# Two-block transformer on one core: mixer preparation reordered, last expert gate turned earlier, sums of squares by column groups

## Chip, cores and metric

The kernel runs on one core of a Trainium2 chip, as one program that computes the whole forward pass. The metric is the device time of one execution in microseconds; the figure of a kernel is the median of its runs. Lower is better.

## What is computed

The input is 512 tokens of width 1024, all in fp32. A first block has two layers (block-sparse attention, then an HGRN2 recurrence), each followed by a mixture of 16 experts with two chosen per token. A second block has, for l = 0 and 1: a gated feed-forward, a mixer of three parts (RWKV-7, sparse latent attention, retention) on one common projection, a second feed-forward. The functions that the change reaches, cut:

```python
# mixture of experts: 512 tokens x 2 experts, sorted by expert, padded to blocks of 128 rows
yb = (silu(xblk @ w1[e]) * (xblk @ w3[e])) @ w2[e]          # gate and up, then down
out = zeros((n + 1, d)).at[buf_t].add(yb * buf_w[:, None])  # back to the tokens
# rms norm ahead of the HGRN2 layer and the others: needs sum(x*x) of every token
y = x * rsqrt(mean(x * x, -1) + eps)
# RWKV-7 (6 heads of 64): low-rank products give decay, a, gate; then a recurrence over tokens
# retention (4 heads of 64), by chunks of 128 tokens
z1, z2 = z[..., :half], z[..., half:]                        # q and k are rotated
rot = concatenate([z1 * cos - z2 * sin, z1 * sin + z2 * cos])
scores = einsum('bnhd,bmhd->bhnm', qc, kc) * intra[None]
inner = einsum('bhnm,bmhe->bhne', scores, vc)
y = y * rsqrt(mean(y * y, -1) + eps); y = silu(g) * y        # per head, then gated
# sparse attention: for every token the 128 best keys by an index score, softmax over them
score = einsum('bqh,bqhs->bqs', iw_b, relu(einsum('bqhd,bsd->bqhs', iq_b, ik)))
_, idx = lax.top_k(where(visible, score, -inf), topk)
```

## The kernel before

**One in-order queue per engine.** The program is written out by hand: each engine (pe = TensorE, act = ScalarE, dve = VectorE, pool = GpSimd, and the DMA queue of SyncE) has one function per stage, which issues its instructions in order, waits for marks that other engines set (`pe.wait_ge(*dve.at(...))`) and sets its own (`.then_inc(*pe.mark(...))`). There is no scheduler: an instruction that waits holds up all behind it on its engine. `edge(eng, name)` (L230) sets a mark of the engine and waits until all the other engines have passed theirs of that name. PSUM banks go round in rings: `take` hands out a bank, and `before` lists what has to have emptied it.

**Weaving.** Where two parts of the work are independent, each is a generator, and `weave` (L2662) calls them in turn, one step each, in the order in which they are given; a generator given as `beside` is advanced once every `every` turns, and what is left of it is taken up later. The same weave stands in the functions of all three engines, so that their queues have the same order.

**Precision.** Matrices are multiplied as sums of three fast products: each operand is split into a rounded part (hi, by ScalarE: `cut_hi` L328, `moe_hi` L1310) and a remainder (lo, by VectorE: `cut_lo` L338, `moe_lo` L1317), and TensorE adds hi*hi, lo*hi and hi*lo (L357 to L359, L1423 to L1425, L1441 to L1443). Weights stream from HBM, three pieces ahead.

**The expert stages** (`moe_pe` L1346, `moe_act` L1498, `moe_dve` L1577). The chosen rows lie in NB = 23 blocks. In step t of the loop TensorE turns the rows of block t, turns the gated product of block t-2 (`turn_a`: four transposes into a bank), runs gate and up of block t-1, and then the down product of block t-2 (`down`, 24 products of 512 columns in four quarters k). In the last step, t = NB + 1, only `turn_a(NB - 1)` and `down(NB - 1)` are left. ScalarE and VectorE walk through the pieces of weights (i counts them in a step) and insert their other work at given i: x_hi, a_hi (L1521), y (L1534, empties the down product), silu; and x_lo, a_lo (L1711), gated (L1717). After the last block y is stored, GpSimd gathers the rows of every token (L1774), VectorE mixes them into four groups of 128 tokens (L1747), TensorE turns each group with eight transposes (L1465), and VectorE adds them to x (L1753, eight instructions of 128x512, from the last group on).

**Sums of squares ahead of the HGRN2 layer** (`hg_sums_pe` L1833, `hg_sums_act` L1846, `hg_proj_act` L1906). ScalarE squares each of the eight 128x512 parts of x (L1855). TensorE multiplies each in four 128x128 blocks with a single column of ones, 32 pairs of weight load and product in all, each shown as two records (L1842 x64), and gets the sum of a token in one of 128 rows; ScalarE takes the root (L1909).

**The mixer** (`mix_pe`, `mix_act`, `mix_dve` L3778 to L3808). It has six parts in order:

- Projections (`mix_proj_*` from L2712): 26 products with streamed weights in `m.order` (27 in mixer 1), one per step s. The index scores and the choice of the keys (`index_*` L2986 to L3059) are woven in, `m.pace[s]` steps of their generator after each projection. VectorE shifts RWKV's projections by one token (`shifted`), two steps after each; at the end it passes the edge "shift", and only then takes what is left of the choice (L3054 to L3059 are its last instructions).
- Preparation: `rwkv_in_*` (L3200) and `ret_*` (L2869) woven together, RWKV first. For RWKV: tanh and sigmoid of the low-rank inputs (L3268, L3269), the nine low-rank products (L3227, outer loop over the three kinds j on their 32 or 64 rows, inner loop over three parts i), the sums of kk squared, cumulative decays, four exponentials of them on ScalarE, among them E3 of the decay less its last step (L3326 on VectorE makes that difference), turned copies and a bonus (L3248). For retention: four rotation products into the ring ps6 (L2876), VectorE's rotation (L2952), scores (L2890) and their decay (L2970), values (L2903), the squares' sums and root, a factor that ScalarE copies wide (L2939) and TensorE spreads (L2686 x16), and two closing products on VectorE (L2983).
- Heads (`head_*` from L3397, first product L3416): three pairs of heads woven together in 16 turns, with one step of the attention (`dsa_*` L3061) every two turns.
- Chunks (`chunks_*` L3543): 27 turns of the RWKV recurrence, woven with the rest of the attention while it lasts.
- Output (`mix_out_*` L3680).

The lines of the steps on the shift edge and the weave:

```python
            edge(dve, n + " shift")                  # in mix_proj_dve, at its end
            for _ in side:                           # side: what is left of the choice
                pass
...
            weave(rwkv_in_dve(v, m), ret_dve(v, m))  # in mix_dve
            edge(dve, m.name + " heads")
```

## Time and profile before

| | |
|---|---|
| median of 3 runs | 4387.55 us (4386.54 to 4388.22) |
| the profiled execution's own time | 4376.6 us |
| its span | 4374.8 us |
| mean granted TensorE clock | 0.966 |
| TensorE busy | 4126.4 us, 94% |
| VectorE busy | 2631.0 us, 60% |
| ScalarE busy | 1965.7 us, 45% |
| GpSimd busy | 167.7 us, 4% |
| DMA | 635.88 MB, 145 GB/s in the mean |

The span runs from the first to the last instruction of the profiled execution; its own time is 1.8 us longer, and the median of the unprofiled runs 10.95 us above that. The granted clock is TensorE's, as a share of full speed: 1.0 is 2.4 GHz, 0.5 is 1.2 GHz. In the rows PE is TensorE's matmul, PEld its weight load, DVE is VectorE, ACT ScalarE, POOL GpSimd; L3219 is line 3219 of the kernel. "x <- y" after a wait names who released it. Times of rows are microseconds from the start of the span unless marked ns.

### The profile page before, as it was taken

The numbers are of one execution on the slowest core, as the hardware profiler recorded it, in microseconds if no ns is written. First come the engines' busy times: TensorE is split into PE (matmuls) and PEld (weight loads), VectorE is DVE, ScalarE is ACT, GpSimd is POOL, SyncE is SP. The second block draws the span as 40 slices with busy tenths as digits, with TensorE's granted clock in tenths as the row PEclk, the third lists the DMA queues.
The fourth block names the chain that finished last, engine by engine and source line by source line (L and its number), as shares of the span: only waits on it lengthen the run. The fifth ranks groups of instructions, "written<-read, shape, count | busy, mean of one in ns | idle before, by whom it ended". The sixth has DMA issues, their size and how long they took to land.

```text
span 4374.8 us, 61152 instructions
## 1 busy us (share of the span) xinstructions
PE 4126.4 (94%) x25548; PEld 3197.4 (73%) x25548; DVE 2631.0 (60%) x4330; ACT 1965.7 (45%) x3254; POOL 167.7 (4%) x151
## 2 busy tenths in 40 slices
PE   7889999998998999989999978999999999889998
PEld 4656778886777788867777656777777776567776
DVE  4467669995346599964445865544544457655444
ACT  3345448884345488852223343322322233443222
POOL 0000000000011000010000000000000000000000
PEclk9999999998999999989999989999999999899999
DMA  5155269994210599942222101222222221012221
GB/s 206 63 193 188 78 256 426 414 403 159 87 59 2 232 426 410 407 170 97 94 87 101 45 3 40 96 95 83 94 98 86 85 107 44 2 40 78 96 96 68
DMA packets 61853, 635.88 MB, mean 145 GB/s; under 512 B 6743, under 2 KB 7127, under 8 KB 27016
## 3 DMA queue, kind: packets, MB, share of 16 engines
q1 hardware_dynamic: 46024, 575.34, 33.4%
q0 software_dynamic: 8928, 32.51, 2.0%
q10 hardware_dynamic: 6624, 24.12, 1.4%
q8 instruction: 201, 3.29, 0.3%
q14 instruction: 76, 0.62, 0.0%
HBM read 601.49 MB, written 30.45 MB: 144 GB/s over the span
## 4 chain that ended last, share of the span: by engine, by line
PE 83%; DVE 9%; ACT 5%; issue 1%; DMA 1%; POOL 0%; POOLq 0%; SPq 0%; DVEq 0%; ACTq 0%
PE ps L357 14%; PE ps L358 14%; PE ps L359 14%; PE ps L1425 4%; PE ps L1424 4%; PE ps L1423 4%; PE ps L1441 2%; PE ps L1443 2%; PE ps L1442 2%; PE ps L1013 2%; DVE wbuf_r L338 1%; PE ps L573 1%; PE ps L378 1%; PE ps L379 1%; PE ps L380 1%
## 5 line engine op out<-in xcount | busy, mean ns | idle before, releaser
L358 PE MATMUL ps<-arena_r,wbuf_r 128*128 128x512 f32 x2848 | 1139.4, 400 | 0.0
L338 DVE TENSOR_TENSOR wbuf_r<-slot,wbuf_r 128x512 fp32r<-128x512 f32 (+1 forms) x832 | 594.6, 722 | 675.6 <-ACT wbuf_r L328 666.7
L357 PE MATMUL ps<-hT_r,wbuf_r 128*128 128x512 f32 x2144 | 868.7, 405 | 17.9 <-DVE arena_r L475 12.2
L359 PE MATMUL ps<-hT_r,wbuf_r 128*128 128x512 f32 x2144 | 853.3, 398 | 0.0
L328 ACT ACTIVATE wbuf_r<-slot 128x512 fp32r<-128x512 f32 (+1 forms) x832 | 506.4, 614 | 714.0 <-PE ps L359 605.0
L358 PEld LDWEIGHTS ps<-arena_r,wbuf_r 128*128 128x128 f32 x2848 | 537.2, 189 | 134.7 <-issue 4.6
L357 PEld LDWEIGHTS ps<-hT_r,wbuf_r 128*128 128x128 f32 x2144 | 405.6, 189 | 143.1 <-DVE arena_r L475 20.7
L359 PEld LDWEIGHTS ps<-hT_r,wbuf_r 128*128 128x128 f32 x2144 | 406.1, 189 | 101.5
L357 PE MATMUL ps<-arena_r,wbuf_r 128*128 128x512 f32 x704 | 279.1, 396 | 0.0
L359 PE MATMUL ps<-arena_r,wbuf_r 128*128 128x512 f32 x704 | 279.1, 396 | 0.0
L1317 DVE TENSOR_TENSOR wbuf_r<-arena,wbuf_r 128x1024 fp32r<-128x1024 f32 x164 | 195.7, 1221 | 44.3 <-ACT wbuf_r L1310 43.8
L1317 DVE TENSOR_TENSOR arena_r<-arena,arena_r 128x1024 fp32r<-128x1024 f32 x164 | 196.8, 1226 | 5.9 <-ACT arena_r L1310 5.2
L2497 ACT ACTIVATE arena_r<-arena 128x512 fp32r<-128x512 f32 x88 | 55.6, 632 | 309.6 <-DVE arena L2533 309.6
L1310 ACT ACTIVATE wbuf_r<-arena 128x1024 fp32r<-128x1024 f32 x164 | 174.1, 1063 | 44.2 <-PE ps L1425 25.2
L1310 ACT ACTIVATE arena_r<-arena 128x1024 fp32r<-128x1024 f32 x164 | 171.3, 1064 | 36.1 <-PE ps L1425 19.2
L2492 ACT ACTIVATE arena<-arena 128x512 f32<-128x512 f32 x88 | 55.6, 632 | 237.8 <-DVE arena L2527 237.8
L1317 DVE TENSOR_TENSOR wbuf_r<-slot,wbuf_r 128x1024 fp32r<-128x1024 f32 x112 | 133.7, 1221 | 38.4 <-ACT wbuf_r L1310 38.2
L359 PEld LDWEIGHTS ps<-arena_r,wbuf_r 128*128 128x128 f32 x704 | 132.6, 188 | 32.4
L357 PEld LDWEIGHTS ps<-arena_r,wbuf_r 128*128 128x128 f32 x704 | 132.6, 188 | 32.4
L1423 PE MATMUL ps<-wbuf_r,hT_r 128*128 128x512 f32 x368 | 148.4, 403 | 3.1 <-DVE hT_r L1706 3.1
L1310 ACT ACTIVATE wbuf_r<-slot 128x1024 fp32r<-128x1024 f32 x112 | 118.8, 1063 | 70.5 <-DMA slot<-in_moe 45.4
L1425 PE MATMUL ps<-arena_r,hT_r 128*128 128x512 f32 x368 | 146.1, 397 | 0.0
(541 smaller groups left out, 7072.7 us busy)
## 6 DMA issues: line engine op xcount, KB each, us to landing
arena<-in_moe SPq DMA_DIRECT2D x82, 2048.0 KB, 11.3
slot<-in_moe SPq DMA_DIRECT2D x54, 2048.0 KB, 11.7
slot<-in_gu SPq DMA_DIRECT2D x44, 2048.0 KB, 7.5
slot<-in_ada SPq DMA_DIRECT2D x20, 2048.0 KB, 7.6
slot<-in_down SPq DMA_DIRECT2D x16, 2048.0 KB, 7.5
slot<-in_win SPq DMA_DIRECT2D x12, 2048.0 KB, 7.6
yrow<-arena ACTq DMA_DIRECT2D x46, 512.0 KB, 10.5
slot<-in_hgrn SPq DMA_DIRECT2D x8, 2048.0 KB, 7.9
```

The source lines that it names most:

```text
L328: a.activation(hi[:, 0:w], src[:, off:off + w], ACT.Copy).then_inc(*act.mark(c.name, "hi", i))
L338: v.tensor_tensor(lo[:, 0:w], src[:, off:off + w], hi[:, 0:w].bitcast(F32), ALU.subtract) \
L357: p.matmul(bank, hi[:, cs], rh[:, k, :], start=k == 0, stop=False, skip_group_check=True)
L358: p.matmul(bank, hi[:, cs], rl[:, k, :], start=False, stop=False, skip_group_check=True)
L359: t = p.matmul(bank, lo[:, cs], rh[:, k, :], start=False, stop=k == kt - 1, skip_group_check=True)
L1013: t = p.matmul(o, pb[:, half, k * 128:k * 128 + 128], att.diag[u % 2][:, half, :], start=True, stop=True, skip_group_check=True)
L1310: a.activation(hi, src[:, j * 1024:j * 1024 + 1024], ACT.Copy).then_inc(*act.mark(n, "hi", *piece))
L1317: v.tensor_tensor(lo, src[:, j * 1024:j * 1024 + 1024], hi.bitcast(F32), ALU.subtract) \
L1423: p.matmul(bank, xh[:, ks], hi[:, cs], start=k == 0, stop=False, skip_group_check=True)
L1424: p.matmul(bank, xl[:, ks], hi[:, cs], start=False, stop=False, skip_group_check=True)
L1425: t = p.matmul(bank, xh[:, ks], lo[:, cs], start=False, stop=k == 7, skip_group_check=True)
L1441: p.matmul(bank[hf], ah[:, ks], hi[:, cs], start=k == 0, stop=False, skip_group_check=True)
```

## The change

1. `edge` is split: `others_at` only waits. In a mixer VectorE sets its own "shift" mark ahead of its work for the last projection, at s = len(m.order) - 1, and waits for the others' where it did before. What is left of the choice of keys is handed on and woven beside the preparation on VectorE.
2. In the preparation retention comes first and RWKV second, on all engines. The rotation products go to the two banks of the ring `hold`, two and two, a step apart. The low-rank products have the parts i outside and the kinds j inside; tanh and sigmoid of their inputs move to step 20 of the projections. The sums of kk squared come one step earlier. The exponential E3 and VectorE's difference for it are gone: `ah` is computed from E1, shifted by one token inside each chunk of 64, by two instructions. Buffers move (`m.vmix` in three parts, `m.rR`), and with `m.vmix` one product of VectorE becomes three in mixer 1.
3. The end of retention (ScalarE's wide copy, the spread on TensorE, VectorE's closing products) becomes a generator of its own, `ret_end_*`, two steps chained ahead of the attention, beside the heads.
4. In the expert stages the gate of the last block is turned at k == 2 of the down product of the block before; its a_hi and a_lo follow at i == 9 of step t = NB.
5. After each of the first three token groups TensorE runs four products of 128 columns whose result is not used.
6. The sums of squares ahead of HGRN2 become eight products with a 32-column matrix of ones, each into the 32-row group k % 4 of one bank, the first four starting and the last four adding; ScalarE copies the bank, and four products with one column each (`corners`) add the four groups for every token.

```diff
 def edge(eng, name):
     eng.also("edge", name)
+    others_at(eng, name)
+
+def others_at(eng, name):
     for other in (pe, act, dve, pool):
...
 # moe_pe: down(b), and the loop over t
     for k in range(4):
+        if b == NB - 2 and k == 2:
+            turn_a(b + 1)
...
-    if 0 <= t - 2:
+    if 0 <= t - 2 < NB - 1:
         turn_a(t - 2)
...
     for dt in range(8):
         p.transpose(out[dt][:, t4 * 128:t4 * 128 + 128], ...)
+    if t4 < 3:
+        busy_pe(p, out[7][:, 384:512], 4)
 # moe_act (moe_dve the same with a_lo)
-    if i == 2 and t > 1:
+    if i == 2 and 1 < t <= NB:
         a_hi(t - 2)
+    if i == 9 and t == NB:
+        a_hi(t - 1)
 # hg_sums_pe
+    bank = hg.ps.take("rows", (act, "hgrn", "x rows"))
...
+    for k in range(8):
+        c = k % 4 * 32
+        pe.wait_ge(*act.at("hgrn", "x sq", k))
+        p.matmul(bank[c:c + 32, :], ones[:, 0:32], m.xg[k // 2 % 2][:, k % 2 * 512:k % 2 * 512 + 512], start=k < 4,
+                 stop=k > 3, ...).then_inc(*pe.mark("hgrn", "x sums", k))
...
-    for k in range(8):
-        pe.wait_ge(*act.at("hgrn", "x sq", k))
-        for t4 in range(4):
-            at = k % 2 * 512 + t4 * 128
-            t = p.matmul(bank[:, t4:t4 + 1], m.xg[k // 2 % 2][:, at:at + 128], ones[:, 0:1], ...)
+    pe.wait_ge(*act.at("hgrn", "x rows"))
+    for t4 in range(4):
+        t = p.matmul(bank[:, t4:t4 + 1], m.gsb[1][:, t4 * 128:t4 * 128 + 128], corners, start=True, stop=True, ...)
+    t.then_inc(*pe.mark("hgrn", "x col"))
 # hg_proj_act
     act.wait_ge(*pe.at("hgrn", "x sums", 7))
+    a.activation(m.gsb[1], hg.ps.buf("rows"), ACT.Copy).then_inc(*act.mark("hgrn", "x rows"))
+    act.wait_ge(*pe.at("hgrn", "x col"))
 # mix_plan
-    m.rR = m.rot.rearrange("p a b -> p (a b)")
+    m.rR = hflat[:, 1536:2560]
...
-    m.vmix, m.vdiff = m.bon, vfirst
+    m.vmix, m.vdiff = [hT[:, 6, :], hT[:, 7, :], late[:, 3584:4096]], vfirst
 # mix_proj_act
+    if s == 20:
+        act.wait_ge(*dve.at(n, "shifted", 9))
+        a.activation(m.lo[0:32, :], m.lo[0:32, :], ACT.Tanh).then_inc(*act.mark(n, "lo", 0))
+        a.activation(m.lo[64:128, :], m.lo[64:128, :], ACT.Sigmoid).then_inc(*act.mark(n, "lo", 2))
 # mix_proj_dve
+    if s == len(m.order) - 1:
+        dve.also("edge", n + " shift")
...
-    edge(dve, n + " shift")
-    for _ in side:
-        pass
+    others_at(dve, n + " shift")
+    return side
 # ret_pe (ret_dve yields at the same places)
     for z in range(4):
-        bank = m.ps6.take(("rot", z), (dve, n, "rot", z))
+        bank = m.hold.take(("rot", z), (dve, n, "rot", z))
...
-    yield
+        if z % 2:
+            yield
...
+def ret_end_pe(p, m):
     for i in range(2):
-        bank = m.ps6.take(("ret spread", i), (dve, n, "ret done", i))
+        bank = m.dps.take(("ret spread", i), (dve, n, "ret done", i))
...
         pe.wait_ge(*act.at(n, "ret R"))
         spread_pe(p, bank, m.rR, 2, i).then_inc(*pe.mark(n, "ret spread", i))
     yield
+    yield
 # rwkv_in_pe (rwkv_in_act the same)
-    for j, rows in ((1, slice(32, 64)), (0, slice(0, 32)), (2, slice(64, 128))):
-        for i in range(3):
+    for i in range(3):
+        for j, rows in ((1, slice(32, 64)), (0, slice(0, 32)), (2, slice(64, 128))):
...
-    yield
     bank = take("kk sums", (act, "kk root"))
...
+    yield
 # rwkv_in_act: Tanh, Sigmoid and this go
-    act.wait_ge(*dve.at(n, "less"))
-    a.activation(m.ah, m.ah, ACT.Exp, scale=-rate).then_inc(*act.mark(n, "E3"))
 # rwkv_in_dve
-    tt(m.ah, m.cum, m.lw, ALU.subtract, n, "less")
...
-    dve.wait_ge(*act.at(n, "E3"))
-    v.scalar_tensor_tensor(out=m.ah, in0=m.kkn, scalar=-1.0, in1=m.ah, op0=ALU.mult, op1=ALU.mult)
+    v.scalar_tensor_tensor(out=by_chunk(m.ah)[:, :, 1:64], in0=by_chunk(m.kkn)[:, :, 1:64], scalar=-1.0,
+                           in1=by_chunk(m.E1)[:, :, 0:63], op0=ALU.mult, op1=ALU.mult)
+    v.tensor_scalar(by_chunk(m.ah)[:, :, 0], by_chunk(m.kkn)[:, :, 0], -1.0, None, ALU.mult)
 # mix_pe (mix_act and mix_dve alike)
-    weave(rwkv_in_pe(p, m), ret_pe(p, m))
+    weave(ret_pe(p, m), rwkv_in_pe(p, m))
     edge(pe, m.name + " heads")
-    dsa = dsa_pe(p, m)
+    dsa = chain(ret_end_pe(p, m), dsa_pe(p, m))
     weave(*[head_pe(p, m, i) for i in range(3)], beside=dsa, every=2)
 # mix_dve
-    weave(rwkv_in_dve(v, m), ret_dve(v, m))
+    weave(ret_dve(v, m), rwkv_in_dve(v, m), beside=choice)
```

## Rows read from the trace of the kernel before

**Rows 1.** The page, part 1: busy us, share of the span, instructions

```profile
PE 4126.4 (94%) x25548; PEld 3197.4 (73%) x25548; DVE 2631.0 (60%) x4330; ACT 1965.7 (45%) x3254; POOL 167.7 (4%) x151
```

**Rows 2.** Preparations: us, then busy PE, PEld, DVE, ACT, POOL; PEclk, DMA share, GB/s

```profile
2499.00:2569.70 70.70, 58.29 (x216) 31.64 (x217) 41.68 (x66) 33.02 (x46) 0.00 (x0) 0.70 0.04 16
...
3703.80:3780.50 76.70, 63.72 (x222) 33.16 (x222) 45.81 (x64) 33.70 (x48) 0.00 (x0) 0.68 0.04 14
```

**Rows 3.** Waits (total us, times, longest): TensorE, whole run; VectorE, preparation 0; 1

```profile
PE ps L3219 <- DVE arena L3056: 10.8, 2, 6.6
...
DVE arena L2952 <- PE ps L2876: 13.7, 1, 13.7
DVE wbuf L2970 <- PE ps L2890: 6.6, 5, 2.6
...
DVE arena L2979 <- ACT arena L2936: 2.0, 1, 2.0
...
DVE wbuf L2970 <- PE ps L2890: 8.0, 4, 4.5
```

**Rows 4.** Order of time on TensorE, mixer 0: start us, us, line, xcount

```profile
2500.02 12.77 PE L3227 MATMUL ps<-arena,small 32*128 32x512 f32 x18
2512.72 6.39 PE L2876 MATMUL ps<-arena,const 128*128 128x512 f32 x8
...
2532.21 1.97 PE L2903 MATMUL ps<-wbuf,arena 128*64 128x512 f32 x4
```

**Rows 5.** Order of time, mixer 0: what the change takes out or moves

```profile
2527.98 1.76 DVE L3326 TENSOR_TENSOR slot<-slot,arena 128x1536 f32<-128x1536 f32 x1
...
2568.87 0.69 DVE L2983 TENSOR_TENSOR hT<-hT,ps 128x512 f32<-128x512 f32 x1 [1.02 <-PE ps L2686]
...
2565.05 3.78 PE L2686 MATMUL ps<-const,arena 128*128 128x128 f32 x16 [1.74 <-ACT arena L2939]
```

**Rows 6.** Order of time: bonus products of both mixers; ScalarE pieces, table load

```profile
2539.95 2.84 PE L3248 MATMUL ps<-arena,const 128*128 128x512 f32 x6
...
3748.54 5.43 PE L3248 MATMUL ps<-arena,const 128*128 128x512 f32 x6 [3.71 <-DVE arena L3364]
...
2475.49 0.63 ACT L328 ACTIVATE wbuf_r<-slot 128x512 fp32r<-128x512 f32 x1 [2.19 <-PE ps L359]
...
2499.60 1.28 ACT L3269 ACT_TABLE_LOAD   x1
```

**Rows 7.** Busy time by stretch: mixer 0, heads, chunks with attention, chunks after it

```profile
2569.70:2637.40 67.70, 54.38 (x2192) 45.45 (x2192) 42.28 (x104) 26.36 (x61) 0.00 (x0) 1.00 0.04 8
2637.40:2690.50 53.10, 50.67 (x504) 37.36 (x504) 29.70 (x83) 24.56 (x67) 0.00 (x0) 1.00 0.09 36
2690.50:2702.10 11.60, 6.57 (x216) 5.70 (x212) 6.99 (x15) 1.00 (x2) 0.00 (x0) 1.00 0.01 1
```

**Rows 8.** Last expert of stage 0 in order of time; page row L1317

```profile
1013.10 0.68 DVE L1717 TENSOR_TENSOR arena<-arena,ps 128x512 f32<-128x512 f32 x1
...
1020.33 0.77 PE L1441 MATMUL ps<-wbuf_r,arena_r 128*128 128x512 f32 x1 [3.50 <-DVE arena_r L1711]
...
1027.45 1.08 ACT L1534 ACTIVATE arena<-ps 128x512 f32<-128x512 f32 x2 [7.99 <-PE ps L1443]
...
1032.61 0.94 POOL L1774 DMA_INDIRECT arena<-yrow,arena  x1 [85.20 <-DMA yrow<-arena]
...
L1317 DVE TENSOR_TENSOR wbuf_r<-arena,wbuf_r 128x1024 fp32r<-128x1024 f32 x164 | 195.7, 1221 | 44.3 <-ACT wbuf_r L1310 43.8
```

**Rows 9.** End of stage 0 in order of time: token groups, squares, spread

```profile
1049.70 5.36 DVE L1753 SCALAR_TENSOR_TENSOR xT<-ps,modv,xT 128x512 f32<-128x512 f32 x8 [0.57 <-PE ps L1465]
...
1049.18 1.97 PE L1465 MATMUL ps<-const,arena 128*128 128x128 f32 x8 [0.72 <-DVE arena L1747]
1051.26 13.79 PE L1842 MATMUL ps<-const,arena 128*128 128x1 f32 x64
1066.43 2.04 PE L1882 MATMUL ps<-arena,const 128*128 128x512 f32 x2 [1.39 <-DVE arena L1964]
```

69 lines of the change are left out of this document (45 added, 24 removed).

## The prediction, on record before the changed kernel was run

> **What bounds the kernel now.** I read the page first: TensorE is busy 94% of the span [rows 1]. So a gain can only come from stretches in which TensorE waits, or runs at half clock, and the change touches three kinds of them. I then took busy times by stretch, the waits of TensorE and VectorE, and the order of time around each edit.
>
> The preparation of a mixer is the largest. It lasts 70.7 us in mixer 0 and 76.7 in mixer 1, at a mean granted clock of 0.70 and 0.68, and VectorE is busy only 41.68 and 45.81 us of it [rows 2]. The waits say why: before it TensorE stands still for the choice of index keys (L3056), 6.6 us in mixer 0 and the other 4.2 of the 10.8 in mixer 1; then VectorE waits 13.7 us for the rotation products (L2876), which stand behind the low-rank ones, and later 6.6 us (8.0 in mixer 1) for the score products (L2890) [rows 3]. The choice ends where the preparation begins, at 2499.0 [rows 2], and then the low-rank products hold TensorE for 12.77 us [rows 4].
>
> **The change part by part.** All sums are against the profiled execution, 4376.6 us (span 4374.8); the median of the runs, 4387.55, is 10.95 above it, and I carry that offset over unchanged.
>
> *The shift edge.* TensorE, ScalarE and the queue that loads the decay table now wait for VectorE only up to its step before the last projections, about 2489. TensorE starts the preparation at about 2493.0 instead of 2499.0 (in mixer 1, 4.2 us of wait less 0.5: 3700.1 instead of 3703.8). VectorE itself gains nothing here: its choice still ends at 2498.9. With the idle time may go the fall of the clock behind it, which the mean of 0.70 over the stretch holds [rows 2].
>
> *The order.* Two rotation products now come ahead of the low-rank ones, in the two hold banks, so VectorE turns q and k right after the choice and its 13.7 us of waiting go. The third rotation product waits for VectorE to empty a bank (about 2500); the low-rank products stand before it and the kk sums behind it, and ScalarE needs until about 2505 for their inputs anyway. The sum for mixer 0, from two queues:
> - VectorE: 41.68 busy, less the removed subtraction (1.76, L3326) and the two closing products that move to the heads (1.38, L2983) [rows 5] = 38.5. From 2499.2 that gives 2537.7 as a floor. Its waits for the scores (6.6) stay, and so do those for ScalarE's root (2.0) and squares (an estimated 0.6) [rows 3]: 2546.9.
> - TensorE: 58.29 busy [rows 2], less the moved spread 3.78 [rows 5] = 54.5 at the same mix of clocks; from 2493.0: 2547.5. The low-rank products may overlap more (below, up to 4 us): 2543.5.
> Both queues hand work to each other several times (scores, kk spread, bonus, turns), so neither floor is reached; I take 4 us above the higher: 2551 against 2569.7, -18.7. Mixer 1 in the same way: VectorE 45.81 - 3.14 = 42.7 from 3704.0 gives 3746.7 plus 8.0 and 2.6 of waits = 3757; TensorE 63.72 - 3.78 from 3700.1 = 3760, less 4, plus 6 of handing over: 3762 against 3780.5, -18.5. Bounds: TensorE at full clock throughout. Six bonus records take 2.84 us at full clock and 5.43 at half [rows 6], so every TensorE term shrinks by up to 1.9; the chain is then VectorE's floor plus its closing waits, 2544.5 and 3753.5, -25 and -27. TensorE at half throughout: its 54.5 become some 68, 2562 and 3774, -8 and -7.
>
> *Removed in it:* one exponential on ScalarE and its wait; both lay beside VectorE's work and are counted nowhere. The negated product becomes two instructions, one over 8 chunks' first columns: +0.2 on VectorE, inside the 4 us. Tanh and sigmoid (0.63 each, as a record of 512 columns takes, and a table load of 1.28 [rows 6]) move into the projections at step 20. ScalarE idles 2.19 us before each weight piece there [rows 6] and is three pieces ahead, so 2.5 to 3.8 us of it are hidden: 0. If not, TensorE would stop for at most that, +3.8 per mixer.
>
> *Low-rank order.* With j inside i, products on rows 32 to 64, 0 to 32 and 64 to 128 follow each other. That rows or columns of different groups run side by side the trace shows: four records of L2903 (64 columns each half) take 1.97 us, where eight records of L2876 take 6.39 at the same clock [rows 4]. So nine products may fall from 12.77 towards 9 us. ScalarE empties them at some 0.65 us each (its 512-column records take 0.63 [rows 6]), 5.9 us; both lie ahead of VectorE's need of them (about 2509), so only the 4 us above hang on it. The Trainium skill, "TensorEngine Tiling (Array Packing)", section Key Properties, speaks against this edit: a change of tiling mode drains the engine, and here the 32-row and the 64-row forms alternate three times. By that rule the products would stay near 12.8 us at half clock, mixer ends would move by up to 4 us each, and the total would be 4350; no row here separates the drain from the clock.
>
> *The end of retention moves beside the heads.* Factor spread (3.78 at half clock), ScalarE's copy and two closing products no longer stand before the heads, but take the first two steps of the attention that is woven in. Sixteen turns of the heads hold 8 such steps; attention is now two steps later throughout. In the heads TensorE is busy 54.38 of 67.7, so 13 us of gaps are there for 1.9 us of spread at full clock, while two attention steps (about 2 us) leave. In the chunks TensorE is busy 50.67 of 53.1: full. Twenty turns of 2.65 us with attention are followed by seven of 1.66 us (11.6/7) [rows 7]; two more turns become long: +2.0. Sum +2.5 per mixer, +5.0; bounds 0 and +9 (3.78 + 2 x 2.65, nothing hidden).
>
> *Last expert's gate turned inside the product ahead (two stages).* Now TensorE turns it behind that product and waits 3.50 us for a lo (L1711), since ScalarE cuts three pieces and empties y first; the clock falls, and the first record behind the wait takes 0.77 us [rows 8]. In the new place, halfway through the product (1013.46), the gate is ready at 1013.78 + 0.15: a stall of 0.5. ScalarE then copies it after the first cut, until 1015.2, VectorE's remainder of it ends at 1016.0, and the remainders of the three pieces behind, 1.22 us each, at 1017.6, 1018.8 and 1020.0, each ahead of its use (1018.7, 1020.1, 1021.5). What is queued behind the new waits: the cuts, y of the expert before and its store, 1.2 us later, but 4 ahead of the last store. So 3.50 - 0.5, plus six records at half clock, each an estimated 0.2 us further from the next (1.3; eight in the second stage, 1.5): 4.3 + 4.5 = -8.8. The last y, its store, the gathers and the mixing follow one another [rows 8], so all of it counts. Bounds -6 and -9.5.
>
> *Fillers between the token groups.* Four 128-column products, 1.0 us at full clock: an estimate, half of the 1.97 that eight records of L1465 take at half clock, into gaps of which the last is 0.72 [rows 9]. If they hold the clock, the group ahead ends 0.9 sooner and the gap covers them; the gain is 0.3 per stage at most, since VectorE's updates set the pace. If they don't, each of the last two adds 1.97 - 0.72, 2.5 together. I take 0; ends -1 and +5 for both stages.
>
> *Sums of squares.* 64 records of L1842 take 13.79 us, all on the chain [rows 9]. New: eight products of 32 columns, each in its own column group. VectorE feeds them every 0.67 us (8 in 5.36 from 1049.70) and a square takes 0.6, so the last is there at 1055.8; its two passes at half clock take 2.04 as in L1882: 1057.9; a 0.6 copy (two of L1534 take 1.08); four columns at 8 x 0.215 = 1.7: root at 1060.4 instead of 1065.1, -4.7. The Trainium skill, "TensorE: Matmul & The Clock Gate", in its table of practical rules, gives 2.38 times for three such products at once. By it the products would take 8 x 1.7 / 2.38 = 5.7 us (an estimate), less than the 6.6 in which the squares come, so the sum by it is the same. If they run one after another it is +2.3. Ends -6.5 and +2.3.
>
> Sum: -18.7 - 18.5 + 5.0 - 8.8 - 4.7 = -45.7: 4330.9 profiled, **4342 us** as a median.
>
> **Rivals.**
> - *TensorE stays at half clock in both preparations*: VectorE is now the later queue, TensorE waits for it more often, and the mean of the stretch is only 0.70 even now [rows 2]. Ends 2562 and 3774: -15, +5, -13.5: 4364. Against: 128-row products open the stretch, and no 6.6 us gap does. 13%.
> - *VectorE's floor is reached*: full clock, 2544.5 and 3753.5; heads hide all: -52 + 1 - 9 - 6: 4322. 12%.
> - *Slower*: the attention steps come with a half clock in the heads. The 54.4 us of TensorE work in a heads stage run at 1.00 now [rows 7], but the stage would begin out of a stretch in which TensorE waits for VectorE. At half throughout it costs up to 50 us each, 100 in all: 4440. It decides from about half of both stages on. Against: the heads begin out of such a stretch now, too, and show 1.00. 3%.
> - *It doesn't do what it says*: the choice was already woven into the projections and all its steps but one stay there; if the edge that TensorE waits for still comes behind the choice, the order alone saves some 10 us a mixer: 4360 at worst, or nothing measurable where the heads give it back. 4%.
>
> **How the numbers follow.** Forecast 68%. A measurement of this kernel can tell about 0.2%, 8.8 us. Below 4378.8 lie the forecast, the first two rivals and half of the last: faster 0.94, same 0.03, slower 0.03. The range takes the unknown costs of the forecast and half of each rival beside it: 4323 to 4364.
>
> **What would show it.** TensorE's wait before the preparation under 1 us; VectorE's wait for L2876 gone; the first head product at about 2551 - 13.5 = 2537 on the new time axis, the other gains being ahead of it; the preparation some 52 us after VectorE's last choice step; no 3.50 us before L1441; the root of the sums 9 to 10 us after the last token group. Wrong if the preparation is over 60 us, if heads and chunks grow by over 5 us, or if the 32-column products start one after another.

## The result, and the profile after

The changed kernel takes **4323.68 us** (median of 4 runs, 4321.76 to 4325.24) against 4387.05 before (4 runs, 4375.48 to 4388.22): the ratio is 0.9869, with a 95% interval from 0.9853 to 0.9885. The forecast was 4342, with a range from 4323 to 4364, so the time lies 0.7 us inside the lower bound. The profiled execution takes 4325.24 us (span 4323.4), 51.4 less than the one of before, where the prediction's sum was 45.7.

The page: TensorE is busy 28.9 us less than in [rows 1], and the mean granted clock is 0.976 instead of 0.966. Of both spans that makes 2 x 0.034 x 4374.8 = 297 us at half clock before and 2 x 0.024 x 4323.4 = 208 now.

```profile
PE 4097.5 (95%) x25556; PEld 3176.7 (73%) x25556; DVE 2624.1 (61%) x4332; ACT 1965.8 (45%) x3257; POOL 165.9 (4%) x151
```

The stretches of mixer 0 (preparation, heads, chunks) and of the preparation of mixer 1. Columns as in [rows 2]:

```profile
2477.40:2532.60 55.20, 44.89 (x203) 23.18 (x203) 46.01 (x79) 28.79 (x43) 0.00 (x0) 0.84 0.06 20
2532.60:2599.20 66.60, 54.45 (x2172) 46.09 (x2172) 39.35 (x96) 24.80 (x55) 0.00 (x0) 0.95 0.02 4
2599.20:2669.70 70.50, 64.47 (x750) 48.23 (x750) 40.22 (x107) 28.18 (x75) 0.00 (x0) 0.98 0.09 31
3666.10:3723.40 57.30, 46.28 (x206) 22.56 (x207) 47.17 (x73) 29.10 (x45) 0.00 (x0) 0.88 0.06 19
```

The preparation is now measured from the first rotation product, 0.73 us behind the projections. VectorE's waits, first in mixer 0, then in mixer 1: the 13.7 us for the rotation products of [rows 3] are gone, and those for the scores are 5.0 and 6.3:

```profile
DVE wbuf L3008 <- PE ps L2917: 5.0, 5, 2.1
DVE arena L3017 <- ACT arena L2967: 1.7, 1, 1.7
...
DVE wbuf L3008 <- PE ps L2917: 6.3, 4, 4.5
```

The order of time at the end of the projections of mixer 0 and after them, VectorE, ScalarE and TensorE (answers to [rows 4]):

```profile
2451.06 1.29 DVE L342 TENSOR_TENSOR wbuf_r<-slot,wbuf_r 128x512 fp32r<-128x512 f32 x2 [3.56 <-ACT wbuf_r L332]
...
2484.83 0.43 DVE L3099 TENSOR_SCALAR arena<-arena 128x512 f32<-128x512 f32 x1
2485.39 0.69 DVE L2989 TENSOR_TENSOR arena<-ps,arena 128x512 f32<-128x512 f32 x1
...
2446.50 1.28 ACT L2794 ACT_TABLE_LOAD   x1
2447.80 0.63 ACT L2794 ACTIVATE arena<-arena 32x512 f32<-32x512 f32 x1
2448.44 1.28 ACT L2795 ACT_TABLE_LOAD   x1
2449.74 0.63 ACT L2795 ACTIVATE arena<-arena 64x512 f32<-64x512 f32 x1
...
2477.44 1.96 PE L2902 MATMUL ps<-arena,const 128*128 128x512 f32 x4 [0.73 <-PE ps L363]
2479.24 0.60 PE L3266 MATMUL ps<-const,arena 128*128 128x128 f32 x4
2479.76 6.40 PE L3274 MATMUL ps<-arena,small 32*128 32x512 f32 x18
2486.14 1.12 PE L2902 MATMUL ps<-arena,const 128*128 128x512 f32 x2
2488.26 1.13 PE L2902 MATMUL ps<-arena,const 128*128 128x512 f32 x2 [0.99 <-DVE arena L2989]
```

TensorE has all nine low-rank products behind it at 2486.16, while VectorE finishes the choice at 2485.26 (L3099) and turns q and k right behind it (L2989). From there to the first head product at 2532.58 VectorE is busy 38.5 of 47.3 us, and its named waits are the 5.0, 1.7 and 0.6 us for the scores, the root and the squares. TensorE is busy 37.1 us of it, so VectorE's chain sets the pace.

The last expert of stage 0 (answers to [rows 8]); in the place of the wait of 3.50 us stands one of 0.21:

```profile
1013.95 0.66 PE L1411 MATMUL ps<-const,arena 128*128 128x128 f32 x4 [0.21 <-DVE arena L1727]
...
1014.65 0.60 ACT L1529 ACTIVATE arena_r<-ps 128x512 fp32r<-128x512 f32 x1 [1.15 <-PE ps L1411]
...
1015.28 0.69 DVE L1721 TENSOR_TENSOR arena_r<-ps,arena_r 128x512 fp32r<-128x512 f32 x1 [0.25 <-ACT arena_r L1529]
...
1023.00 1.08 ACT L1542 ACTIVATE arena<-ps 128x512 f32<-128x512 f32 x2 [3.54 <-PE ps L1449]
...
1029.65 0.94 POOL L1786 DMA_INDIRECT arena<-yrow,arena  x1 [82.11 <-DMA yrow<-arena]
```

The end of that stage (answers to [rows 9]):

```profile
1046.23 1.09 PE L1471 MATMUL ps<-const,arena 128*128 128x128 f32 x8
1048.16 5.76 PE L1853 MATMUL ps<-arena,const 128*32 128x512 f32 x16 [0.84 <-ACT arena L1873]
1054.70 1.02 PE L1860 MATMUL ps<-tiny,arena 128*128 128x1 f32 x8 [0.78 <-ACT arena L1927]
...
1053.95 0.60 ACT L1927 ACTIVATE arena<-ps 128x512 f32<-128x512 f32 x1 [1.14 <-PE ps L1853]
1055.76 0.26 ACT L1929 ACTIVATE tiny<-ps,tiny 128x4 f32<-128x4 f32 x1 [1.21 <-PE ps L1860]
```

Where the 51.4 us come from, by the times of the same instructions in both traces: the end of expert stage 0 with the sums 9.3, the HGRN2 layer 0.5, expert stage 1 5.9, mixer 0 from the end of its projections to its output product 16.7, the way to the next mixer 1.8, mixer 1 19.6; the rest gives 2.4 back.

### The profile page after: what moved, and what is told of

The parts are those of the page before. It is cut to its first block, busy times and chain, and to the rows that moved or that the text cites. A ratio compares the mean times of both kernels' runs of the same rounds, so it can differ in the third digit from the quotient of the medians.

```text
span 4323.4 us, 61177 instructions
## 1 busy us (share of the span) xinstructions
PE 4097.5 (95%) x25556; PEld 3176.7 (73%) x25556; DVE 2624.1 (61%) x4332; ACT 1965.8 (45%) x3257; POOL 165.9 (4%) x151
## 4 chain that ended last, share of the span: by engine, by line
PE 81%; DVE 11%; ACT 5%; issue 1%; DMA 1%; POOL 1%; POOLq 0%; SPq 0%; DVEq 0%; ACTq 0%
PE ps L361 14%; PE ps L362 14%; PE ps L363 14%; PE ps L1429 4%; PE ps L1427 4%; PE ps L1428 4%; PE ps L1449 2%; PE ps L1447 2%; PE ps L1448 2%; DVE wbuf_r L342 2%; PE ps L1017 2%; PE ps L577 1%; PE ps L382 1%; PE ps L383 1%; PE ps L384 1%
## 5 line engine op out<-in xcount | busy, mean ns | idle before, releaser
L361 PE MATMUL ps<-hT_r,wbuf_r 128*128 128x512 f32 x2144 | 869.2, 405 | 19.3 <-DVE arena_r L479 13.6
```

The costliest lines, as they stand in the source:

```text
L361: p.matmul(bank, hi[:, cs], rh[:, k, :], start=k == 0, stop=False, skip_group_check=True)
```

## The experiments

A single execution can't settle a few microseconds here. u_gate below takes over 9 us longer up to the last y of the two expert stages, and yet its span is 3.5 us under that of the changed kernel: code common to both, at 15 to 27 us, already ended 3.6 us sooner, and the clock fell at other moments. So the runs are read by the lengths of stages, and where the clock fell beside them. In the table "choice" is the end of the choice of keys and "prep" the first head product, both from the end of the projections; then the lengths of heads and of chunks (to the first output product), all from the one profiled execution of each kernel, in us, mixer 0 / mixer 1. A name with u_ is the changed kernel with one part (in u_both two) undone, one with i_ a further try on top of it.

| kernel | median (ratio to before, interval) | choice | prep | heads | chunks |
|---|---|---|---|---|---|
| before | 4387.05 | 6.5 / 4.1 | 77.3 / 80.9 | 66.1 / 67.1 | 66.4 / 66.4 |
| changed | 4323.68 (0.9869, 0.9853 to 0.9885) | 8.6 / 5.3 | 55.9 / 58.0 | 66.6 / 67.9 | 70.6 / 68.9 |
| u_gate | 4325.73 (0.9876, 0.9857 to 0.9896) | 8.6 / 5.4 | 56.3 / 58.0 | 67.0 / 68.3 | 70.6 / 68.9 |
| u_fill | 4321.09 (0.9865, 0.9846 to 0.9884) | 8.6 / 5.3 | 55.4 / 58.2 | 67.4 / 69.3 | 68.9 / 68.9 |
| u_sums | 4326.43 (0.9868, 0.9849 to 0.9887) | 8.6 / 5.4 | 55.1 / 58.2 | 67.3 / 68.8 | 68.9 / 68.9 |
| u_lora | 4328.53 (0.9877, 0.9860 to 0.9893) | 8.6 / 5.4 | 55.0 / 64.8 | 67.3 / 65.9 | 69.0 / 68.9 |
| u_edge | 4328.96 (0.9875, 0.9859 to 0.9892) | 8.5 / 5.3 | 60.0 / 65.1 | 68.7 / 64.9 | 68.9 / 68.9 |
| u_order | 4330.30 (0.9890, 0.9866 to 0.9914) | 8.5 / 5.3 | 57.5 / 63.1 | 69.1 / 67.1 | 69.0 / 68.9 |
| u_both | 4356.22 (0.9940, 0.9916 to 0.9964) | 8.5 / 5.3 | 70.7 / 81.2 | 67.1 / 68.1 | 68.9 / 70.5 |
| u_end | 4337.26 (0.9892, 0.9874 to 0.9909) | 8.5 / 5.3 | 60.7 / 63.7 | 67.8 / 69.1 | 70.9 / 70.5 |
| u_tanh | 4320.28 (0.9851, 0.9823 to 0.9879) | 6.5 / 4.1 | 53.8 / 57.9 | 67.7 / 67.9 | 68.9 / 68.9 |
| i_tanh | 4319.87 (0.9848, 0.9818 to 0.9877) | 6.5 / 4.1 | 53.8 / 58.0 | 68.2 / 67.6 | 68.9 / 68.9 |
| i_all | 4325.03 (0.9865, 0.9837 to 0.9894) | 6.5 / 4.1 | 52.5 / 60.8 | 69.8 / 66.7 | 70.4 / 68.9 |
| u_e3 | 4324.36 (0.9860, 0.9831 to 0.9889) | 8.6 / 5.4 | 56.6 / 59.5 | 67.6 / 69.3 | 68.9 / 70.5 |

u_gate, u_fill and u_sums don't touch the mixers: their preps of mixer 0 and the changed kernel's, 55.1 to 56.3 in four executions (58.0 to 58.2 in mixer 1), show what a prep can be read to. The kernel before was run beside each group of four; its medians were 4381.65, 4384.11 and 4386.26, so that medians of different groups are compared by their ratios.

**u_gate: the last expert's gate where it was.**

```diff
-                    if b == NB - 2 and k == 2:
-                        turn_a(b + 1)
...
-                if 0 <= t - 2 < NB - 1:
+                if 0 <= t - 2:
                     turn_a(t - 2)
...
-                    if i == 9 and t == NB:
-                        a_hi(t - 1)
```

> The changed kernel with one part undone: the last expert's gate is turned behind the down product ahead of it again, and its a_hi and a_lo come at i == 2. My theory: TensorE again waits about 3.5 us before the last down product in both expert stages, the clock falls behind each wait, and the stages end 4.0 to 4.5 us (first) and 4.5 to 5.7 us (second) later than in the changed kernel, +8.5 to +10 us in all; the fillers between the token groups change nothing of that. Rival: the store and the gathers behind the last product don't follow it (in the first stage the gathers come only 2.96 us earlier in the changed kernel, though the last product ends 4.4 us earlier), so that undoing it costs some 3 us a stage, +6.

```profile
1015.34 0.76 PE L1445 MATMUL ps<-wbuf_r,arena_r 128*128 128x512 f32 x1 [3.50 <-DVE arena_r L1717]
```

From the last turned row block to the last y (ScalarE's emptying of the down product) it is 45.28 and 45.56 us before (stages 0 and 1), 40.71 and 40.70 in the changed kernel and, within 0.01, in each of the eleven others that keep the part, 45.30 and 45.55 here. The part is worth 4.6 and 4.9 us. What follows doesn't shrink with it for sure: from the last y to the first token group it is 12.8 to 15.0 us in stage 0 over all executions (12.3 to 13.1 in stage 1), 14.7 in the changed kernel, 13.3 here, 13.2 before. The chain of waits shows where the first 1.5 us of that went: the last store's landing, first in the kernel before and then in the changed one.

```profile
1028.57 3.32 DMA yrow<-arena
```

```profile
1024.11 4.81 DMA yrow<-arena
```

So theory and rival both hold a part: 4.6 us at the product, of which one profiled execution showed 3.0 at the gathers.

**u_fill: no fillers between the token groups.**

```diff
-                if t4 < 3:
-                    busy_pe(p, out[7][:, 384:512], 4)
```

> The changed kernel without the four 128-column products after each of the first three token groups. My theory, by the prediction's sum: 0, at most +1 in all. Rival: they are what keeps TensorE at full clock from 1043.5 to 1057.2, where it was at half before. Then without them the stretch from the token groups to the first projection of the HGRN2 layer runs at half clock: the last turned group takes 1.97 instead of 1.09 us, the sixteen records of 32 columns of rows take longer than 5.76, and the spread (1.81) and the first records of the projection too, +2 to +4 in the first expert stage, and about +1 to +2 in the second, where only the feed-forward's first products follow.

The root comes 9.67 us behind the last token group instead of 9.53. Around the token groups of stage 0 the clock is at half for 10.2 us, where the twelve executions with fillers have 0 to 6.8 (6.8 in the changed kernel), and in stage 1 for 30.7 us instead of 20.5 (17.1 to 23.9 in the others). In stage 0 it is still at half until 1045.5, in the first 3.9 us of the eight 32-column products (1041.62 to 1047.38), and even so they take 5.76 us, as at full clock: the squares pace them. None of the lengths grows by more than 1 us, and the median is not above the changed kernel's. The theory holds: in this execution the clock is at half for longer, and nothing is lost by it that can be measured.

**u_sums: one column for each block again.**

```diff
-            bank = hg.ps.take("rows", (act, "hgrn", "x rows"))
...
+            for k in range(8):
+                pe.wait_ge(*act.at("hgrn", "x sq", k))
+                for t4 in range(4):
...
+                    t = p.matmul(bank[:, t4:t4 + 1], m.xg[...][:, at:at + 128], ones[:, 0:1], ...)
```

> The changed kernel with the sums of squares as 32 pairs of a 128x128 load and a one-column product again; fillers and all else stay. My theory: 64 records behind the squares; at the full clock that the fillers now give some 64 x 0.12 = 7.5 us of records, so that the root comes less late than before: +1 to +2.5 us. Rival (the change's own gain is in the form of the product and not in the clock): 64 records at 0.215 us, 13.8 us, root 14.6 us or more behind the last token group instead of 9.5: +4.7 to +6.4.

```profile
1046.99 1.09 PE L1471 MATMUL ps<-const,arena 128*128 128x128 f32 x8 [0.62 <-DVE arena L1759]
1048.91 12.55 PE L1854 MATMUL ps<-const,arena 128*128 128x1 f32 x64 [0.83 <-ACT arena L1867]
...
1061.50 0.27 ACT L1921 ACTIVATE tiny<-ps,tiny 128x4 f32<-128x4 f32 x1 [6.20 <-PE ps L1854]
```

From the last token group to the root: 14.51 us, 15.90 before and 9.53 in the changed kernel. My theory fails and the rival stands: the form of the product is worth 5.0 us. The other 1.4 us go with the clock, which in u_sums was granted in full from 1043.4 to 1050.3 and before was at half from 1043.6 on; the fillers alone don't make them, since without them (u_fill) the root comes only 0.14 us later. The clock fell at 1050.3, 1.4 us behind the first one-column product, and the 64 records took 12.55 us, not 7.5.

**u_lora: the low-rank products in the old order.**

```diff
-            for i in range(3):
-                for j, rows in ((1, slice(32, 64)), (0, slice(0, 32)), (2, slice(64, 128))):
+            for j, rows in ((1, slice(32, 64)), (0, slice(0, 32)), (2, slice(64, 128))):
+                for i in range(3):
```

> The changed kernel with the low-rank products in the order of before (kinds j outside, parts i inside), on TensorE and ScalarE. In the changed kernel 18 records take 6.40 us at full clock, where they took 12.77 at half, just the factor of two. My theory: the order alone gives nothing, the 18 records take 6.4 us (within 0.5) in either order; but the scans on VectorE wait for the decay's three parts (j = 0), which now come after three instead of eight of the nine products, so mixer ends move by less than 1 us each: 0 to +1. Rival A (row groups side by side): with the old order the records take 8 us or more, +1.5 or more per mixer where VectorE waits for them. Rival B (changing the row group drains the engine): the old order is faster on TensorE, under 6 us.

The nine products in u_lora, mixer 0 and mixer 1:

```profile
2478.80 6.58 PE L3274 MATMUL ps<-arena,small 32*128 32x512 f32 x18
...
3665.61 9.51 PE L3274 MATMUL ps<-arena,small 32*128 32x512 f32 x18
```

And four records in narrow windows, first the changed kernel's first two 32-row products (2480.2:2480.7), then what was in flight in u_lora at 2480.1:2480.4 (by chance the two rows have the same numbers):

```profile
2479.76 1.13 PE L3274 MATMUL ps<-arena,small 32*128 32x512 f32 x4
```

```profile
2479.76 1.13 PE L3274 MATMUL ps<-arena,small 32*128 32x512 f32 x4
```

In mixer 0 both orders take nearly the same, 6.40 and 6.58: the order alone gives 0.2 us. The starts of the single records say why. In the new order the two 32-row products of each part run side by side (four records start at 2479.76, 2479.77 and twice at 2480.30), so that all twelve 32-row records go in pairs, but every step to the next start takes 0.52 to 0.54 us. In the old order the two kinds of 32 rows overlap, too: the last four records of the first kind start at 2479.76, 2480.19, 2480.62 and 2481.05, the first four of the second at 2479.76, 2480.30, 2480.73 and 2481.16. Eight of the twelve go in pairs, and the steps inside a kind take 0.43 us, but for 0.53 behind its first record and 0.52 from the last 32-row to the first 64-row one. So Rival A's side by side and Rival B's price of a change are both at work and cancel.

The trace of before has the same pairs at half clock (2501.89 twice, then 2502.74 and 2502.91): what the new order was to bring was there in good part already. The 6.4 us against 12.77 [rows 4] are the clock. In mixer 1 of u_lora it fell at 3669.0, in the last of the twelve 32-row records, the products took 9.51 us, and the preparation 6.8 us more. In the ten executions with the new order and the moved edge it never fell during these products; one fall in two mixers of the old order doesn't show that the order is what keeps it.

**u_edge, u_order, u_both: the two edits that bring the rotations forward.**

```diff
# u_edge
-                if s == len(m.order) - 1:
-                    dve.also("edge", n + " shift")
...
-            others_at(dve, n + " shift")
+            edge(dve, n + " shift")
# u_order (act and dve alike); u_both has both edits
-            weave(ret_pe(p, m), rwkv_in_pe(p, m))
+            weave(rwkv_in_pe(p, m), ret_pe(p, m))
```

> The changed kernel with the shift edge where it was: VectorE sets its mark behind its last step of the choice in the projections, so TensorE and ScalarE start the preparation some 8 us later (in mixer 0 at about 2485.3 instead of 2477.4). My theory: the preparation is now bound by VectorE, which begins at the same time as before; the rotation products come first, so it waits 1 us for the first and has the inputs of its scans (due at 2496) in time: +1 to +4 us per mixer, 2 to 8 in all. Rival: the whole chain of ScalarE (gates, kk root, exponentials) moves with the edge: +8 in mixer 0 and +5 in mixer 1.

> The changed kernel with the two generators of the preparation in the order of before (RWKV first, then retention), all other parts as changed. The prediction put the 13.7 us of VectorE's wait for the rotation products down to the order. Theory now, from the trace after: with the edge moved, TensorE has the low-rank products behind it at 2484.5, before the choice ends (2485.3), and the rotations follow at once, so that the order is worth under 2 us per mixer: 0 to +4 in all. Rival (the prediction's): the order is what takes the wait away, and without it 6 us or more of it come back in each mixer, +12.

> The changed kernel with the edge and the order undone together. Theory: each of the two hides the low-rank products from VectorE alone; without both they stand again between the choice and the rotations, with the clock fallen behind the idle time: VectorE waits 7 (full clock) to 14 us (half) for the first rotation, +8 to +14 us per mixer, 16 to 28 in all, more than the sum of the two undone one by one. Rival: the two are worth their sum, at most +12.

Mixer 0 in order of time, u_edge, then u_order, then u_both with VectorE's wait:

```profile
2488.43 3.71 PE L2900 MATMUL ps<-arena,const 128*128 128x512 f32 x4 [8.69 <-DVE arena L3097]
2491.98 0.60 PE L3264 MATMUL ps<-const,arena 128*128 128x128 f32 x4
2492.51 6.40 PE L3272 MATMUL ps<-arena,small 32*128 32x512 f32 x18
```

```profile
2477.15 6.40 PE L3274 MATMUL ps<-arena,small 32*128 32x512 f32 x18
2483.48 1.98 PE L2902 MATMUL ps<-arena,const 128*128 128x512 f32 x4
```

```profile
2481.29 1.09 PE L3264 MATMUL ps<-const,arena 128*128 128x128 f32 x4 [8.69 <-DVE arena L3097]
2482.31 12.09 PE L3272 MATMUL ps<-arena,small 32*128 32x512 f32 x18
2494.33 3.49 PE L2900 MATMUL ps<-arena,const 128*128 128x512 f32 x4
...
DVE arena L2987 <- PE ps L2900: 13.2, 1, 13.2
```

Against the changed kernel the preps grow by 4.1 and 7.0 us in u_edge, by 1.6 and 5.1 in u_order, and by 14.9 and 23.2 in u_both: 38.1 us in all, against 17.8 for the two one by one. VectorE's waits for rotation products go the same way: 5.4 and 7.3 us in u_edge, 0 and 5.0 in u_order, 13.2 and 20.8 in u_both, where the changed kernel has none above 0.1. So the prediction's account of the order falls: each edit alone keeps most of the low-rank products out of VectorE's way, the edge by running them under the choice, the order by running them behind the first rotations. Only without both does the wait of before come back, in mixer 0 with 8.7 us of standing still and 12.09 us of low-rank products at half clock; in mixer 1 the clock is at half for 41 us on end (3678.4 to 3719.4).

The kind of effect came out as expected before u_both, the sizes did not: 38.1 us lie above its 16 to 28. u_edge's 11.1 us lie above its theory (2 to 8) and nearer to the 13 of its rival, and u_order's 6.7 lie between its theory (0 to 4) and its rival (12).

**u_end: the end of retention back in the preparation.**

```diff
-            dsa = chain(ret_end_pe(p, m), dsa_pe(p, m))
+            dsa = dsa_pe(p, m)          # the body of ret_end_* follows in ret_*, bank from ps6
```

> The changed kernel with the end of retention back in the preparation (wide copy, spread and two closing products behind the root, attention chained without it). Prediction: the preparation grows by the copy (1.1), the spread (1.9 at full clock, 3.8 at half) and the closing product behind it (0.7), +4 to +6.5 per mixer, and heads and chunks give back 2 to 3.5 (the two attention steps fall into the full chunks): net +1.5 to +4 per mixer. Rival: the heads had room for the attention's steps anyway, and nothing comes back in the chunks: +4 to +6.5 per mixer.

The preps grow by 4.9 and 5.7 us, as both said. Of the 2 to 3.5 us that heads and chunks were to give back nothing shows in this execution: together they take 138.7 and 139.6 us, against 137.2 and 136.8 in the changed kernel, so that from the projections to the output product the two mixers are 6.4 and 8.5 us longer. By the numbers the expected +1.5 to +4 fails, and the rival's +4 to +6.5 is nearer.

The clock stands beside it. In u_end's chunks it fell for 10.2 us in mixer 0 (2604.3 to 2614.5) and for 6.8 in mixer 1. Kernels with the part in the heads take 68.9 to 69.0 us there without a fall and 70.4 to 70.6 where it fell for 3.4, and the kernel before, without the part and without a fall, takes 66.4. Less half the length of the falls u_end's chunks are 65.8 and 67.1 us. So the two shifted steps cost some 2.5 us, by the kernel before and by this correction; that they come back when the part is undone no run shows, and whether the undoing brought on the falls is open. The median is 13.6 us above the changed kernel's.

**u_tanh and i_tanh: tanh and sigmoid back in the preparation, or late in the projections.**

```diff
# u_tanh: the three lines at s == 20 go back to the start of rwkv_in_act; i_tanh:
-                if s == 20:
+                if s == len(m.order) - 1:
```

> The changed kernel with tanh and sigmoid of the low-rank inputs back at the start of the preparation on ScalarE. The prediction costed the move to step 20 at nothing. The trace after shows otherwise: there the two and their two table loads hold ScalarE for 3.9 us, VectorE waits 3.56 us for the next weight piece (before: 0.6 at most), and the choice ends 8.6 us behind the projections instead of 6.4. Theory: undone, the choice ends 2 us sooner in mixer 0, and since VectorE bounds the preparation, that is shorter by 2 us, less what the later low-rank products cost (ScalarE has 9 us of slack before the scans): -1 to -2 in mixer 0, -1 to +2 in mixer 1, where the choice ends only some 2 us behind the projections. Rival: the later products delay VectorE, +3 per mixer.

> The changed kernel with tanh and sigmoid five steps later (six in mixer 1), at the last but one step of the projections, behind the last weight piece and in ScalarE's 5.06 us of idle time before the last projection. Theory: VectorE's wait of 3.56 us goes and the low-rank inputs are still there when the projections end: the preparation is 2 us shorter in mixer 0 and 0.5 to 2 in mixer 1, 2.5 to 4 in all. Rival: the choice is not delayed by that wait but by its own length, 0.

i_tanh's ScalarE in mixer 0:

```profile
2474.48 0.61 ACT L2794 ACTIVATE arena<-arena 32x512 f32<-32x512 f32 x1
2475.11 1.28 ACT L2795 ACT_TABLE_LOAD   x1
2476.40 0.63 ACT L2795 ACTIVATE arena<-arena 64x512 f32<-64x512 f32 x1
```

VectorE's waits in i_tanh's mixer 1, from 3670 to 3684 (the changed kernel has none there):

```profile
DVE arena L2989 <- PE ps L2902: 1.3, 1, 1.3
```

Both bring the choice back to 6.5 us behind the projections and shorten the prep of mixer 0 by 2.1 us, to 53.8, under all of the undisturbed ones. VectorE's wait of 3.56 us is gone (0.7 at most). In mixer 1 the choice ends 1.3 us sooner and the prep stays at 58.0: VectorE spends the 1.3 us in waiting for the third rotation product, which stands on TensorE behind the nine low-rank ones, and its first scan comes 14.7 us behind the projections in all three. So step 20 was not free in mixer 0, and in mixer 1 i_tanh's 0.5 to 2 us didn't come. The medians are 3.4 and 3.8 us under the changed kernel's, more than the 2.1 us of this stage, and the intervals overlap.

**i_all: constants out of the preparation and two idle products.**

```diff
# mix_proj_dve: the copies of masks, us, ui at step 4 of mixer 0; gone from rwkv_in_dve
+                if s == 4 and m.l == 0:
...
# ret_pe, before the third rotation, and rwkv_in_pe, before the sums of kk
+                if z == 2:
+                    busy_pe(p, bank, 1)
...
+            busy_pe(p, bank, 1)
```

> As i_tanh, and two more edits: the five copies of constants on VectorE (mixer 0 alone, 1.7 us with their gaps) move from the preparation to step 4 of the projections; and two idle products of 1.0 us each go before the third rotation and before the sums of kk, where TensorE waits 1 us each and the clock falls at 2490.8. Theory: VectorE bounds the preparation, so the copies give 1.7 us in mixer 0; the idle products hold the clock over the sums and scores, which spares VectorE up to 2 us of its wait for the scores: 1.5 to 4 us shorter than i_tanh in mixer 0, 0 to 2 in mixer 1. Rival: the sums' products with two columns let the clock fall all the same, and in mixer 1 the idle product delays the rotation by 1 us: -1.7 and +1.

Mixer 1 on TensorE, i_all and then i_tanh:

```profile
3672.83 1.12 PE L392 MATMUL ps<-const 128*128 128x512 f32 x2
3673.79 1.88 PE L2912 MATMUL ps<-arena,const 128*128 128x512 f32 x4
...
3678.37 1.12 PE L392 MATMUL ps<-const 128*128 128x512 f32 x2
3679.33 3.99 PE L2698 MATMUL ps<-const,hT 128*128 128x2 f32 x24
```

```profile
3675.57 1.99 PE L2902 MATMUL ps<-arena,const 128*128 128x512 f32 x4
...
3680.25 2.84 PE L2698 MATMUL ps<-const,hT 128*128 128x2 f32 x24
```

In mixer 0 the prep is 1.3 us shorter than in i_tanh, about the copies; in mixer 1 it is 2.8 longer. There TensorE didn't idle where the idle products went. They delay the third rotation by 1.0 us and the sums of kk by 1.9; the clock fell 17.2 us behind the projections (3680.6), much as in i_tanh (16.9 us, 3683.1), but now while the sums ran, and these took 3.99 us instead of 2.84. The rival is nearer: it had -1.7 and +1 where -1.3 and +2.8 were measured. With a median of 4325.03 it is no gain.

**u_e3: the difference and the third exponential back.**

```diff
+            tt(m.ah, m.cum, m.lw, ALU.subtract, n, "less")
...
+            a.activation(m.ah, m.ah, ACT.Exp, scale=-rate).then_inc(*act.mark(n, "E3"))
...
```

> The changed kernel with VectorE's difference (1.76 us) and ScalarE's third exponential back. Theory: VectorE bounds the preparation, and its 1.76 us, less 0.2 for the second of the two new instructions, come back in full: +1.5 per mixer, +3 in all. Rival: they fall into VectorE's waits for the scores behind them (2.1 and 0.75 us), 0 to +0.5.

The preps are 56.6 and 59.5, that is 0.7 and 1.5 more than in the changed kernel and 0.3 to 1.5 and 1.3 to 1.5 more than in the four executions with the same preparation. The theory holds in mixer 1; in mixer 0 the two can't be told apart.

**What stays open.** The parts don't add up: the growths of the preps in u_both, u_end, u_e3, u_tanh and u_lora come to 17.5 us in mixer 0 and to 37.1 in mixer 1, where the whole change took 21.4 and 22.9 off. The clock, which falls at other places in each of them, is in all of these numbers. The moved buffers, the sums of kk a step earlier and the rotations' change of banks were not undone by themselves.

## Why the prediction was right, and where it was off

- **The sum and the median.** In the profiled executions 45.7 us were forecast and 51.4 measured. The rest of the distance to 4342 is the offset: 10.95 us between the profiled execution and the median of before were carried over unchanged, while the changed kernel's median lies 1.6 under its profiled execution. The one profiled execution of before was among its lowest (all its runs reach from 4368.8 to 4394.6), so the offset belonged to that execution and not to the kernel. That is 12.5 of the 18.3 us of error. So the median lies in the range by 0.7 us, close to the 4322 of the rival "VectorE's floor is reached" (12%), though its preparations did not come: they shrank by 21.4 and 22.9 us, between the forecast's 18.7 and 18.5 and that rival's 25 and 27.
- **The shift edge: right.** TensorE waits 0.73 us in both mixers where 6.6 and 4.2 stood, against 0.6 and 0.5 forecast. "VectorE itself gains nothing here: its choice still ends at 2498.9" missed that another part of the change delays it by 2.1 us.
- **The order: right sum, wrong cause.** 18.7 and 18.5 us were forecast for the two preparations and 21.4 and 22.9 measured. The term that was off are the 4 us (5 to 6 in mixer 1) added for the handing over: from the end of the choice to the heads VectorE's floor with its waits made 47.7 and 53.3, and it measured 47.3 and 52.7. That VectorE's busy time and its waits set the end is borne out (in mixer 0 38.5 us of work left were forecast and measured). That the sum came within 0.6 us is in part luck: in mixer 0 its waits for scores and root were 1.9 us shorter than those carried over, and short gaps of 1.5 us, which the sum left out, stood against them. And that TensorE's queue, as late as VectorE's by the sum (2547.5 and 2546.9), did not hold it up goes with the clock, whose rise was not forecast. The credit given to the order alone is not borne out: with the edge moved it is worth 1.6 and 5.1, and edge and order together 14.9 and 23.2.
- **The clock.** The forecast took the mix of clocks of before. The half-clock rival (13%) fell: the mean rose from 0.70 and 0.68 to 0.84 and 0.88, and TensorE's work in the preparation of mixer 0 fell from 58.3 to 44.9 us, where 54.5, or 50.5 with the overlap, were forecast.
- **Low-rank order: wrong.** The products were to fall from 12.77 to 9 us at half clock; the order gives 0.2 us, the clock the rest. The overlap that was to be gained was already in the 12.77: the trace of before has eight of the twelve 32-row records in pairs. The rule of the Trainium skill ("TensorEngine Tiling (Array Packing)", section Key Properties), that a change of the tiling mode drains the engine, agrees with the trace: across a change nothing starts together, and the first record behind it comes 0.52 us after the last one ahead of it, where 0.43 stands between records of one kind. But the step behind the first record of a new kind is as long, with the mode changed or not, and the drain is not told apart from that.
- **Tanh and sigmoid: wrong.** They were put at 0 since ScalarE idles before each piece and is three ahead. But with two table loads they hold it for 3.9 us, VectorE waited 3.56, and VectorE, still busy with the choice, ends it 2.1 and 1.3 us later. It costs 2.1 us in mixer 0 and nothing in mixer 1, where VectorE would have waited for the third rotation. The cover was looked for on TensorE, but the engine without slack was VectorE.
- **The end of retention: right in direction.** Heads and chunks together grow by 4.7 and 3.3 us (2.5 forecast, 5 the sign of being wrong), 1.7 of the former by a fall of the clock of 3.4 us at 2600. Against that stand the 4.9 and 5.7 us that the preparation saves.
- **The gate: right.** 4.3 and 4.5 forecast, 4.6 and 4.9 measured. "All of it counts" held but for the scatter of the store behind it.
- **Fillers: right**, 0 taken, 0.1 measured. **Sums of squares:** 4.7 forecast, 6.4 measured: the clock was full instead of half, so the last product is over at 1053.9, 7.7 us behind the last group instead of 8.7, and the four columns take 1.02 us instead of 1.7. One sign of being wrong, by its words, did come: the products start one after another, 0.52 to 0.93 us apart, as the squares come. The loss that it stood for didn't, since each takes 1.0 to 1.1 us and not 2. Whether column groups run side by side was hardly tested: only once, at 1052.81 and 1052.87, does a product start within 0.1 us of a pass of the one before.

## What to carry to other kernels

Where two engines pass work to and fro, add up each queue from its own last fixed point with the waits that remain; here VectorE's sum was within 0.6 us, partly because two errors cancelled, and the margin on top made the forecast worse. Before forecasting that products will run side by side, look at the starts of their single records: they may do so already. When two edits hide the same work, undo them together before giving either the credit. And a step that is moved under a busy TensorE is free only if no other engine in that stretch, here VectorE behind ScalarE's pieces, is the one that is late.

## What the runs showed of the hardware

- Two products on different 32-row groups start within 10 ns and run side by side, also when all of one kind is issued ahead of the other. Records of one kind start 0.43 us apart at full clock; the step to a 64-row product and the step behind the first record of a kind take 0.52 to 0.54, some 0.1 us more each.
- With 64 single-column products behind their loads the clock fell 1.4 us after the first (1048.91 and 1050.3), in one execution. With eight 32-column products, fed by the same squares, it never fell during them in twelve executions (full from 1043.7 to 1057.4 in the changed kernel), and in u_fill it rose to full under them.
- The landing of the same 512 KB store took 3.32 us in one execution and 4.81 in another, and from y to the first token group it was 12.8 to 15.0 us over fourteen executions.
- The moments at which the clock falls differ between executions of the same code, and a fall of 3.4 us in the chunks made them 1.4 to 1.7 us longer.
